# Where the sums of squares are added: all additions of the stream's squares on VectorE, GpSimd left with the powers

## The reference

```
def rms_norm(x, g):
    xf = x.astype(jnp.float32)
    y = xf * lax.rsqrt(jnp.mean(xf * xf, axis=-1, keepdims=True) + EPS)
    return (y * g.astype(jnp.float32)).astype(x.dtype)
...
        h = rms_norm(x, mix_norm_g[l])
        x = x + mixer_attn_rglru(h, ...)          # l = 0; pool_mixer(h, ...) for l = 1
        x = x + memory_xattn(rms_norm(x, xattn_norm_g[l]), mem_n, ...)
        x = x + sq_relu_mlp(rms_norm(x, mlp_norm_g[l]), mlp_w1[l], mlp_w2[l])
...
        h = x + 0.5 * swiglu(rms_norm_2(x, ffn1_norm[l]), ...)
        n = rms_norm_2(h, mix_norm[l])
        ...
        h = h + y @ w_out[l]
        h = h + 0.5 * swiglu(rms_norm_2(h, ffn2_norm[l]), ...)
        x = rms_norm_2(h, final_norm[l])
```

## Time and profile before

| | |
|---|---|
| median of 3 runs | 1657.5 us (1657.44 to 1657.68) |
| the profiled execution | 1657.64 us, its span 1656.3 us |
| TensorE busy (matmul) | 1648.4 us |
| VectorE busy | 1193.9 us |
| ScalarE busy | 882.2 us |
| GpSimd busy | 177.1 us |
| mean granted clock of TensorE | 0.999 |

### The profile page before, as it was taken

The page is one execution under the profiler, slowest core; times in us unless marked ns, Lnnn a source line. Parts: engine busy times, 40 slices in busy tenths (PEclk is TensorE's granted clock), DMA queues, the critical chain, the costliest instruction groups (busy, mean ns, idle before and its releaser), DMA issues.

```text
span 1656.3 us, 24699 instructions
## 1 busy us (share of the span) xinstructions
PE 1648.4 (100%) x10328; PEld 1486.6 (90%) x10328; DVE 1193.9 (72%) x1448; ACT 882.2 (53%) x1096; POOL 177.1 (11%) x169
## 2 busy tenths in 40 slices
PE   9999999999999999999999999999999999999998
PEld 8899988888999888888889998888888899998887
DVE  7877487765657777677767877778687677787763
ACT  6665465444555545455554655556555545565543
POOL 0401010011101001200021110003200022010002
PEclk9999999999999999999999999999999999999999
DMA  9444355555434555545565335455555655155551
GB/s 356 164 153 166 115 180 199 182 192 215 154 128 155 196 209 191 198 178 196 204 221 203 106 115 191 179 200 207 186 195 187 237 207 179 52 178 180 196 184 51
DMA packets 42991, 297.39 MB, mean 180 GB/s; under 512 B 4864, under 2 KB 5632, under 8 KB 8448
## 3 DMA queue, kind: packets, MB, share of 16 engines
q1 hardware_dynamic: 39744, 282.87, 47.7%
q10 hardware_dynamic: 3136, 12.95, 2.1%
HBM read 294.75 MB, written 1.05 MB: 179 GB/s over the span
## 4 chain that ended last, share of the span: by engine, by line
PE 99%; DVE 1%; POOL 0%; issue 0%; POOLq 0%
PE ps L369 43%; PE ps L374 22%; PE ps L363 4%; PE ps L364 4%; PE ps L365 4%; PE ps L415 4%; PE ps L416 4%; PE ps L417 4%; PE ps L522 1%; PE ps L542 1%; PE ps L928 1%; PE ps L907 1%; PE ps L619 0%; PE ps L632 0%; PE ps L501 0%; PE ps L885 0%
## 5 line engine op out<-in xcount | busy, mean ns | idle before, releaser
L1632 DVE TENSOR_TENSOR w_lo<-raw,w_hi 128x2048 fp32r<-128x2048 f32 x267 | 610.0, 2289 | 193.4 <-ACT w_hi L1069 190.5
L1069 ACT ACTIVATE w_hi<-raw 128x2048 fp32r<-128x2048 f32 x267 | 507.7, 1904 | 176.6 <-PE ps L374 110.1
L369 PE MATMUL ps<-xT,w_hi 128*128 128x512 f32 x1920 | 467.5, 392 | 0.0
L369 PEld LDWEIGHTS ps<-xT,w_hi 128*128 128x128 f32 x1920 | 350.1, 188 | 66.0 <-issue 0.5
L369 PE MATMUL ps<-hT,w_hi 128*128 128x512 f32 x1194 | 290.0, 391 | 0.0
L374 PEld LDWEIGHTS ps<-xT,w_lo 128*128 128x128 f32 x1920 | 251.9, 191 | 13.1
L374 PE MATMUL ps<-xT,w_lo 128*128 128x256 f32 x1920 | 255.5, 282 | 0.0
L369 PEld LDWEIGHTS ps<-hT,w_hi 128*128 128x128 f32 x1194 | 217.5, 188 | 40.7
L1121 ACT ACTIVATE tmp<-ps 128x512 f32<-128x512 f32 x120 | 71.8, 598 | 245.4 <-PE ps L374 245.4
L2349 POOL TENSOR_TENSOR ff<-ff 128x256 f32<-128x256 f32 x73 | 96.3, 1319 | 950.6 <-ACT ff L1099 661.1
L363 PE MATMUL ps<-xT,w_hi 128*128 128x256 f32 x576 | 167.2, 290 | 0.0
(11 more groups left out here) (285 smaller groups left out, 1737.9 us busy)
## 6 DMA issues: line engine op xcount, KB each, us to landing
raw<-weights_dram SPq DMA_DIRECT2D x263, 1024.0 KB, 4.8
tmp<-third_taps_dram ACTq DMA_DIRECT2D x2, 2048.0 KB, 10.8
raw<-weights_dram SPq DMA_DIRECT2D x4, 768.0 KB, 5.0
raw<-weights_dram SPq DMA_DIRECT2D x4, 512.0 KB, 8.2
tmp<-mem_dram ACTq DMA_DIRECT2D x2, 1024.0 KB, 7.2
x<-x_in_dram SPq DMA_DIRECT2D x2, 512.0 KB, 5.6
arena<-mem_dram ACTq DMA_DIRECT2D x1, 1024.0 KB, 10.4
arena<-pool_mat_dram ACTq DMA_DIRECT2D x1, 1024.0 KB, 6.4
```

What stands on the lines that cost most here:

```text
L369: pe.matmul(ps[:, bank, :].rearrange("p (a n) -> p a n", a=2), b.hi(u, slice(j * P, j * P + P)), src[:, k, :, :], start=first, stop=False)
L1069: act.activation(b.hi(u, slice(0, width(u))), b.raw(u, slice(0, width(u))), ACT.Copy).then_inc(*mark("hi", u))
L1632: dve.tensor_tensor(b.lo(u, cs), b.raw(u, cs), b.hi(u, cs).bitcast(F32), ALU.subtract).then_inc(*mark("lo", u))
```

## The change

All additions of squares move from GpSimd to VectorE. `square_sums` and `joined_sums` go out of GpSimd's program, which keeps the powers. On VectorE three new helpers make the additions. In a down projection the addition of chunk oc - 1 follows the low part of chunk oc; with the last chunk the last two additions come, 6 and 7 (5 and 6 at chunk 6 in the output stage, where TensorE adds the last square itself). In `x_pairs` and in the loop of xat1 they stand between and behind the low parts. The mark "last_sum" goes, since the last addition is now as all others.

```
--- before.py
+++ after.py
-def last_on_vector(f):
-
-    return f == "xat0" or f[:4] == "ffn2"
...
     def stream_sums(f, bank):
         rest = chunks_left(f)
-        pe.wait_ge(*(at("sqsum_x0") if f == "x0" else at("last_sum", f) if last_on_vector(f) else
-                     at("sqsum", f, KC - 1 - len(rest))))
+        pe.wait_ge(*(at("sqsum_x0") if f == "x0" else at("sqsum", f, KC - 1 - len(rest))))
...
+    def add_square(f, c):
+
+        pairs = f in ("xat0", "mlp0", "xat1", "mlp1") or f[:4] == "ffn2"
+        if c < 1:
+            return
+        dve.wait_ge(*at("sq", f, c | 1 if pairs else c))
+        if c > 1:
+            dve.wait_ge(*at("sqsum", f, c - 1))
+        dve.tensor_tensor(b.acc(), b.sq(0) if c == 1 else b.acc(), b.sq(c), ALU.add).then_inc(*mark("sqsum", f, c))
+
+    def add_joined(c):
+
+        f = "ffn1_1"
+        for name, acc, src in (("sq", b.acc(), b.ff[:, 2 + c % 2, :]), ("sq_j", b.acc_j(), b.ff[:, 4 + c % 2, :])):
+            done = mark("sqsum", f, c) if name == "sq" else mark("sqsum_j", c)
+            dve.wait_ge(*(at("sq", f, c) if name == "sq" else at("sq_j", c)))
+            if c:
+                dve.wait_ge(*(at("sqsum", f, c - 1) if name == "sq" else at("sqsum_j", c - 1)))
+                dve.tensor_tensor(acc, acc, src, ALU.add).then_inc(*done)
+            else:
+                dve.tensor_copy(acc, src).then_inc(*done)
+
+    def add_chunks(f, oc):
+
+        last = {"out": 6}.get(f, KC - 1)
+        done = range(oc - 1, oc) if oc < last else range(oc - 1, last + 1)
+        for c in done:
+            if c >= 0:
+                (add_joined if f == "ffn1_1" else lambda c: add_square(f, c))(c)
+
     def x_pairs(f, u0):
...
         add(2)
         low(1)
+        add_square(f, 1)
         add(3)
         low(2)
+        add_square(f, 2)
+        add_square(f, 3)
         low(3)
-        if last_on_vector(f):
-            dve.wait_ge(*at("sqsum", f, KC - 2))
-            dve.wait_ge(*at("sq", f, KC - 1))
-            dve.tensor_tensor(b.acc(), b.acc(), b.sq(KC - 1), ALU.add).then_inc(*mark("last_sum", f))
+        for c in range(4, KC):
+            add_square(f, c)
...
             lows(v + 3)
             if oc is not None and oc < KC - 1 and nxt != "out":
                 x_low(nxt, oc)
+            if oc is not None and (oc < KC - 1 or nxt != "out"):
+                add_chunks(nxt, oc)
...
         if kc >= 3 and kc % 2:
             x_low("xat1", kc - 3)
             x_low("xat1", kc - 2)
+            add_square("xat1", kc - 5)
+            add_square("xat1", kc - 4)
     x_low("xat1", 6)
     x_low("xat1", 7)
+    for c in range(4, KC):
+        add_square("xat1", c)
     key_rows(1, 0, (5, 6))
```

More of the change, by code:

```diff
@@ L2339, in query_roots @@
             power(ss, ss, 2, mark("qroot", l, h))
[L2341 to L2364, removed]
     pool.memset(b.arena[:, 15, 0:512].bitcast(BF16), 0.0).then_inc(*mark("idle_zeros"))
@@ L2399, in gpsimd_program @@
     key_roots(0, 1)
-    square_sums("xat0", True)
     query_roots(0)
-    square_sums("mlp0", True)
-    square_sums("mix1", False)
     root("mix1")
-    square_sums("xat1", True)
     key_roots(1, 0)
@@ L2408, in gpsimd_program @@
     query_roots(1)
-    square_sums("mlp1", True)
     for l in range(2):
         fa, mx, fb = f"ffn1_{l}", f"mix_{l}", f"ffn2_{l}"
[L2412 to L2415, removed]
         memory_root(f"mem2_{l}")
@@ L2423, in gpsimd_program @@
             root(fa)
-        square_sums(mx, False)
         root(mx)
@@ L2434, in gpsimd_program @@
         power(b.stat[:, W_VAR], b.stat[:, W_VAR], 2, mark("root", f"conv{l}"))
-        square_sums(fb, True)
         root(fb)
-    square_sums("out", False)
     root("out")
```

## The result

The changed kernel takes 1674.92 us in the median of four runs (1673.40, 1673.53, 1676.32 and 1679.63), the kernel before 1657.47: 17.5 us or 1.1% slower, ratio 1.011 with a 95% interval of 1.0098 to 1.0122. The forecast was 1669.1, with a range of 1667.2 to 1672.0. So the sign and the five waits were as foretold, and 5.8 us more came on top, with a spread over the runs (6.2 us) that the kernel before does not have (0.3 us over its four).

A forecast was written before the change was run, and what follows sets the result against it. The prediction took TensorE to bound the kernel, busy 1648.4 of 1656.3 us. Five waits of 11.14 us plus 0.5 for restarts gave 11.6 on the 1657.5 median: 1669.1 us, range 1667.2 to 1672.0.

The forecast's parts named there:

- the five waits: TensorE's sums in mix1, ffn1_0, mix_0, ffn1_1, mix_1 wait for additions queued behind w_lo: 2.03 to 2.84 us, together 11.14.
- TensorE has no slack, so each wait is paid in full: Whole kernel: about 0.6 us of TensorE idle in the middle, so no later gap makes up a wait.
- the five restarts: After each of the five waits TensorE's weight load is not ahead of the matmul: 0.1 us each, 0.5 in all.
- VectorE's added work is nearly paid by what GpSimd gives back: VectorE: 89 more additions cost 38 us, some 23 come back from x_lows; net up to +15 us, hidden behind TensorE.
- I side with no fall, but not firmly: Behind the five waits TensorE's clock stays full, since the work before them is dense; cost 0.
- A granted clock below 1 inside the kernel: Sign in the profile after that would show the prediction wrong; no size given.
- Rival (a): The clock falls after one or more waits, most likely ffn1_1's: 1671.8 us for one, up to 1677 for three; chance 0.11.
- The price of a fall, 2.7 us: Loss per clock fall, taken from the kernel's start: 20 matmuls take 7.31 us there against 4.59 later.
- x_pairs: "Room 0.2 to 0.3, cost 0.": In ffn2, the tightest x_pairs stage, the last sum still arrives 0.2 to 0.3 us before TensorE asks; cost 0.
- None of these waits is on a sum of squares or on a low part of the stream: TensorE's list of waits: nothing VectorE or GpSimd does sooner can be worth more than 0.6 us.

The follow-up runs named there:

- Experiments 3 to 5: 3: changed kernel, additions late only in ffn1_1, 1664.07 us; 4: late only in the other four stages, 1670.31; 5: kernel before, five waits for w_lo added, 1666.57.
- Experiment 2: Changed kernel plus 9 to 12 unused matmuls on TensorE in front of each of the five late sums, filling the waits: 1670.00 us.
- experiment 6: Changed kernel with the last additions in front of lows(v + 3), and one w_lo less ahead of both ffn2 feed forwards: 1657.33 us.
- experiment 4: Changed kernel with the last additions in front of lows(v + 3) in ffn1_1 alone, so the four shorter waits stay: 1670.31 us.
- the half-filled wait: Changed kernel with additions late only in ffn1_1, and 6 unused matmuls (1.29 us) in front of that stage's sums: 1661.30 us.

## Why the prediction was wrong

The measured time is 1657.5 + 0.6 (the spreads, less the relief at mlp0) + 11.9 (waits and restarts) + 4.9 (falls, in the median of four runs) = 1674.9. The forecast had 0, 11.6 and 0 for the three terms.

*TensorE has no slack, so each wait is paid in full.* Right: the waits measure 11.4 us, and with the five restarts they cost 11.9 when they are filled; without them the time is back within 0.6.

*VectorE's added work is nearly paid by what GpSimd gives back.* Right: x_low at 0.48 throughout, 2.4 us more of busy time where up to 15 were allowed, and no wait that comes from the amount of it.

*The five waits and their sizes.* Right: 2.03, 2.21, 2.03, 2.84, 2.03 worked out; against the sums' beginnings in the trace of before, shifted by what each earlier stretch had lost, they measure 2.10, 2.28, 2.10, 2.83, 2.10. The 0.07 that four of them have on top lies in the chained additions, two of which take 0.95 us (398.37 above) where 0.88 was worked out. The restart comes behind that, and its 0.1 was right.

*"I side with no fall, but not firmly."* This is the step that failed: the fall of the clock behind the waits was put at nothing, and it cost 4.9 us in the median. (A granted clock below 1 inside the kernel was named as a sign of being wrong, and it is what came.) The argument was that the fall at the kernel's end came after thin work, and that the work before these waits is dense. Experiments 3 to 5 show that density on both sides does not protect: an idle stretch of 1.4 us was followed by a fall in three of eight runs, one of 2.7 us in five of five, and four of 2.1 us gave at least one in all five. Experiment 2 shows that it is the idling: with matmuls of no use in the waits the falls are gone. What decides in a given run whether a fall comes, and which size it has, no run here shows. The Trainium skill (TensorE: Matmul & The Clock Gate, Why this matters for your kernels) warns only of idle gaps longer than any of these; here shorter ones suffice, and the measurement decides. Rival (a) was thus the case that happened, at a chance of 0.11 where the row at the end of the kernel had already shown a fall 2 us after the last matmul. That row deserved more weight, because it was the only one on the question.

*The price of a fall, 2.7 us.* Mis-sized, from the slow start. Measured: 1.7 us for a fall of 3.4 us at the lower clock and 3.1 for one of 6.8, which is half of the slow stretch or a little less. Rival (a) allowed 1671.8 for one; the four runs' 3.4 to 9.6 us over the filled kernel are two to about six of the smaller size (two are seen in the profiled run; for the others it is an estimate from time and clock).

*x_pairs: "Room 0.2 to 0.3, cost 0."* Wrong by some 0.9 us for the two ffn2 stages, which the relief at mlp0 brings down to 0.6. The sum itself was in time by a hair (additions to 998.83, asked for at 998.89), so the chain to the sum was read nearly rightly, though chained additions came 0.53 apart and not 0.43, which ate the room. But behind the additions stand two w_lo, the mean and the diagonal, and the spread that waits for them had no room either. The prediction followed each sum to TensorE and did not follow the queue one step further.

*"None of these waits is on a sum of squares or on a low part of the stream", so the relief of VectorE is worth nothing.* True of the list, but the list leaves out delays of 0.1 us: the doubled x_lows held up TensorE by some 0.3 us at mlp0.

*The spread over runs.* Not forecast. Whether a wait is followed by a fall, and by which size, differs from run to run, so one program has several times.

## What to carry to other kernels

Moving an operation to another engine is decided by what stands in front of it in that engine's queue: here 92 additions on VectorE cost nothing that can be measured in experiment 6, and twelve of them, each behind a w_lo that itself waits for ScalarE, cost 17 us; the idle time for them was there, 1.63 us, on the other side of the same instruction. On a kernel whose TensorE never pauses, price every new wait twice, once by its length and once by the clock that may fall behind it, and look for the price in the variance too. If a wait of two or three microseconds can't be removed, matmuls of no use in it keep the clock, as in experiments 2 and 3; and when one chain has been followed to its consumer, follow the same queue to the next consumer.

## What the runs showed of the hardware

- Idle stretches of TensorE of 1.4 to 2.7 us between dense work were followed, in some or all runs of a program, by a granted clock of 1.2 GHz for 3.4 or 6.8 us, beginning up to 2.3 us after TensorE had resumed (400.2 after 399.37; with the half-filled wait 1180.9 after 1178.6), in one case already 0.2 us before it (702.8 in experiment 4, where the next matmul came at 702.97). They cost 1.7 or 3.1 us, and which of the two differed from run to run.
- A VectorE scalar_tensor_tensor of 128x256 with two SBUF inputs took 0.48 us alone and 0.96 in the median of the kernel before; 55 of its 96 were lengthened, and each of these overlapped an instruction of GpSimd. The weights' tensor_tensor of 2048 elements showed no such doubling: its median is 2.29 us before and after. By the Trainium skill (SBUF — State Buffer, Who interferes with whom) the one that comes first shuts the other out; the trace agrees in so far as all x_lows fell to 0.48 when GpSimd stopped adding.
